# A hybrid RWKV-7 / mixture-of-experts trunk: gate/up weight pieces by rows in place of by columns

## The reference, cut to what matters

```
gate, up = jnp.split(xb @ w_e_in[e], 2, axis=-1)     # xb: 128 x 1024, w_e_in[e]: 1024 x 1024
return (jax.nn.silu(gate) * up) @ w_e_out[e]         # w_e_out[e]: 512 x 1024
```

## Time and profile before

| | us |
|---|---|
| median of 3 runs | 4692.15 (4687.72 to 4694.24) |
| the profiled execution: its time | 4703.23 |
| the profiled execution: its span | 4701.5 |
| expert stage in it: first weight piece issued | 3439.5 |
| expert stage in it: first gate/up matmul | 3478.96 |
| expert stage in it: last down product begins | 4596.52 |

### The profile page before, as it was taken

One profiled execution on the slowest core, in us unless ns is written; L12 is line 12 of the kernel. 1 busy time (PEld: TensorE's weight loads), 2 busy tenths in 40 slices (PEclk: granted clock), 3 DMA queues, 4 the chain that ended last, 5 costly groups with the idle time before them and its releaser, 6 DMA issues.

```text
span 4701.5 us, 91708 instructions
## 1 busy us (share of the span) xinstructions
PE 4270.4 (91%) x36691; PEld 2267.5 (48%) x36691; DVE 1599.4 (34%) x3167; ACT 1308.9 (28%) x2960; POOL 322.2 (7%) x422
## 2 busy tenths in 40 slices
PE   6999999999999999999999999989859999999991
PEld 4455555555555555555555555555434444444440
DVE  3333443343344344433434433332341111111115
ACT  4123333333333333333333333333301111011115
POOL 0000100010000001000000100000000000000004
PEclk8999999999999999999999999999869999999995
DMA  9101000100100100100100100033269999999998
GB/s 309 52 8 35 23 11 24 34 9 16 40 13 9 47 8 13 48 8 13 46 11 8 50 11 8 8 127 125 89 236 398 398 397 398 398 397 398 398 397 327
DMA packets 316735, 628.36 MB, mean 134 GB/s; under 512 B 11602, under 2 KB 96820, under 8 KB 316340
## 3 DMA queue, kind: packets, MB, share of 16 engines
q1 hardware_dynamic: 297908, 555.52, 32.6%
q0 software_dynamic: 11520, 41.95, 2.3%
q10 hardware_dynamic: 6912, 25.17, 1.3%
HBM read 561.75 MB, written 60.84 MB: 132 GB/s over the span
## 4 chain that ended last, share of the span: by engine, by line
PE 85%; issue 6%; DVE 4%; DMA 2%; ACT 2%; SPq 1%; POOL 1%; DVEq 0%; POOLq 0%; ACTq 0%
PE bank L962 38%; PE bank L1296 9%; PE bank L1300 5%; PE bank L1176 5%; PE bank L1326 5%; PE duo L1087 4%; PE bank L1330 2%; PE duo L1076 2%; PE duo L1074 1%; PE duo L1280 1%; ACT xs L1362 1%; PE bank L1019 1%; PE duo L899 1%; DMA yb<-y_s,dix 1%; PE bank L1003 1%
## 5 line engine op out<-in xcount | busy, mean ns | idle before, releaser
L962 PE MATMUL bank<-hT,w 128*128 (+1 forms) x4096 | 1792.6, 594 | 0.0
L962 PEld LDWEIGHTS bank<-hT,w 128*128 128x128 f32 x4096 | 778.1, 191 | 996.5 <-issue 996.5
L1296 PE MATMUL bank<-W,xT 128*128 128x512 f32 x1024 | 447.1, 595 | 2.2 <-DVE xT L2201 1.5
L1362 ACT ACT_TABLE_LOAD x268 | 343.8, 1283 | 21.0 <-DVE ub L1920 14.3
L1296 PEld LDWEIGHTS bank<-W,xT 128*128 128x128 f32 x1024 | 192.8, 191 | 233.7 <-issue 233.7
L1300 PE MATMUL bank<-W,xT 128*64 128x512 f32 x1024 | 241.3, 627 | 40.1 <-issue 40.1
L2207 DVE TENSOR_TENSOR gsig<-bank,gsig 128x512 f32<-128x512 f32 x48 | 33.2, 691 | 709.7 <-ACT gsig L1362 709.7
L727 POOL TENSOR_TENSOR Tm<-Tm,idents 128x512 f32<-128x512 f32 x32 | 40.5, 1267 | 2837.0 <-DVE Tm L1953 2837.0
L1176 PE MATMUL bank<-wo,mT 128*128 128x512 f32 x512 | 233.6, 602 | 0.0
L1326 PE MATMUL bank<-W,aT 128*128 128x512 f32 x512 | 225.1, 592 | 0.0
L1362 ACT ACTIVATE gsig<-bank 128x512 f32<-128x512 f32 x48 | 28.7, 597 | 694.7 <-PE bank L1296 423.9
(11 more groups left out here) (366 smaller groups left out, 5533.9 us busy)
## 6 DMA issues: line engine op xcount, KB each, us to landing
W<-in_w_expert_in_dram SPq DMA_DIRECT2D x128, 2048.0 KB, 21.5
W<-in_w_expert_out_dram SPq DMA_DIRECT2D x64, 2048.0 KB, 21.1
w<-in_w_in_dram SPq DMA_DIRECT2D x64, 512.0 KB, 3.9
adaw<-in_w_ada_dram SPq DMA_DIRECT2D x12, 2048.0 KB, 12.9
y_s<-ysb ACTq DMA_DIRECT2D x48, 512.0 KB, 6.7
xt<-in_x_dram SPq DMA_DIRECT2D x16, 512.0 KB, 8.7
WAc<-rank_s SPq DMA_DIRECT2D x32, 256.0 KB, 3.3
GDc<-rank_s SPq DMA_DIRECT2D x32, 256.0 KB, 3.2
```

The costliest lines, as they stand in the source:

```text
L962: ins = mm(PJ[j % 2][:, :], w[:, j, k, :], hT[:, k, ds(group(i) * G, G)], start=k == 0, stop=k == KT - 1)
L1296: ins = mm(GU[half][:, :], xT[:, slot, k, :], ring_in(parts[0])[:, k, :], start=k == 0, stop=k == KT - 1)
L1362: return nc.scalar.activation(o, i, f, **kw)
```

## The change

Each gate/up piece now holds half of the rows in full width: the first piece rows 0 to 511, the second rows 512 to 1023, 4 KB each. The number of pieces, their size, the order of issue, the ring and its slots stay. PE's order inside `gate_up` follows: with the first piece it runs k tiles 0 to 3 of the gate and then k tiles 0 to 3 of up, with the second piece k tiles 4 to 7 of both. The semaphore of the first piece gets another name.

```diff
-        def ring_in(r):
-            return ring(r).rearrange("p (k n) -> p k n", n=DE)
-        def ring_out(r):
+        def ring_rows(r):
             return ring(r).rearrange("p (k n) -> p k n", n=D)
...
-            def in_half(half):
-                return lambda r, e: (ring_in(r), e_in[0, ds(e, 1), :, half * DE:half * DE + DE]
-                                     .rearrange("e (k p) n -> p (e k) n", p=P))
+            def rows_in(part):
+                rows = slice(part * (D // 2), part * (D // 2) + D // 2)
+                return lambda r, e: (ring_rows(r), e_in[0, ds(e, 1), rows, :].rearrange("e (k p) n -> p (e k) n", p=P))
...
-                for half in range(2):
-                    parts = gate_part(s, half)
+                for part in range(2):
+                    parts = in_part(s, part)
                     for r in parts:
                         pe.wait_ge(ring_sem[r % RING], ring_full(h, r))
                     pe.sem_inc(S["pair_go"])
-                    for k in range(KT):
-                        if len(parts) == 1:
-                            ins = mm(GU[half][:, :], xT[:, slot, k, :], ring_in(parts[0])[:, k, :],
-                                     start=k == 0, stop=k == KT - 1)
...
-                    ins.then_inc(S["gu_done"] if half else S["gate_done"], 1)
+                    for half in range(2):
+                        cols = slice(half * DE, half * DE + DE)
+                        for k in range(KT // 2):
+                            kk_ = part * (KT // 2) + k
+                            if len(parts) == 1:
+                                ins = mm(GU[half][:, :], xT[:, slot, kk_, :], ring_rows(parts[0])[:, k, cols],
+                                         start=kk_ == 0, stop=kk_ == KT - 1)
+                            else:
+                                for lane, r in zip(LANE, parts):
+                                    ins = mm(GU[half][lane, :], xT[:, slot, kk_, lane], ring_rows(r)[:, k, cols],
+                                             start=kk_ == 0, stop=kk_ == KT - 1)
+                    ins.then_inc(S["gu_done"] if part else S["first_rows_done"], 1)
```

More of the change, by code:

```diff
@@ L99, in build @@
         shifted operands gates branch km_step rn_step P_step hats rs_step yc_step post_step conv_step sumsq
-        ln_done rstd tr_done T_act T_dve index_col chain patterns ada_trip pair_go gate_done""".split()
+        ln_done rstd tr_done T_act T_dve index_col chain patterns ada_trip pair_go first_rows_done""".split()
         S = {n: ctx.enter_context(nc.semaphore(n)) for n in names}
@@ L362, in ring_full, with in_part @@
             return 16 * (h * 3 + r // RING + (0 if r % RING in (2, 3) else 1)) + RING_BASE
-        def gate_part(s, half):
+        def in_part(s, part):
             base, j = 12 * (s // 3), s % 3
-            return [base + 4 * j + half] if j < 2 else [base + 7 + 2 * half, base + 8 + 2 * half]
+            return [base + 4 * j + part] if j < 2 else [base + 7 + 2 * part, base + 8 + 2 * part]
         def down_part(s):
@@ L617, in _ @@
             for s in range(6):
-                for half, signal in ((0, "gate_done"), (1, "gu_done")):
-                    for r in gate_part(s, half):
+                for part, signal in ((0, "first_rows_done"), (1, "gu_done")):
+                    for r in in_part(s, part):
                         OWNER[r] = (signal, s)
@@ L639, in fill @@
                 sp.dma_start(*source(r, e)).then_inc(ring_sem[r % RING], 16)
-            def in_half(half):
-                return lambda r, e: (ring_in(r), e_in[0, ds(e, 1), :, half * DE:half * DE + DE]
-                                     .rearrange("e (k p) n -> p (e k) n", p=P))
+            def rows_in(part):
+                rows = slice(part * (D // 2), part * (D // 2) + D // 2)
+                return lambda r, e: (ring_rows(r), e_in[0, ds(e, 1), rows, :].rearrange("e (k p) n -> p (e k) n", p=P))
             def rows_out(r, e):
-                return (ring_out(r), e_out[0, ds(e, 1), :, :].rearrange("e (k p) n -> p (e k) n", p=P))
+                return (ring_rows(r), e_out[0, ds(e, 1), :, :].rearrange("e (k p) n -> p (e k) n", p=P))
             def load_block(h, s, down=True):
-                for half in range(2):
-                    for r, column in zip(gate_part(s, half), experts_of(h, s)):
-                        fill(h, r, column, in_half(half))
+                for part in range(2):
+                    for r, column in zip(in_part(s, part), experts_of(h, s)):
+                        fill(h, r, column, rows_in(part))
                 if down:
@@ L1325, in down @@
                         if len(parts) == 1:
-                            ins = mm(Y2[j][:, :], aT[:, slot, k * P:k * P + P], ring_out(parts[0])[:, k, cols],
+                            ins = mm(Y2[j][:, :], aT[:, slot, k * P:k * P + P], ring_rows(parts[0])[:, k, cols],
                                      start=k == 0, stop=k == DE // P - 1)
@@ L1329, in down @@
                             for lane, r in zip(LANE, parts):
-                                ins = mm(Y2[j][lane, :], aT[:, slot, k * P:k * P + P][:, lane], ring_out(r)[:, k, cols],
+                                ins = mm(Y2[j][lane, :], aT[:, slot, k * P:k * P + P][:, lane], ring_rows(r)[:, k, cols],
                                          start=k == 0, stop=k == DE // P - 1)
```

## The result

The changed kernel takes 4650.73 us (median of 4 runs, 4647.93 to 4656.95) against 4693.19 us before (4 runs): ratio 0.9912, 95% interval 0.9899 to 0.9925. In two later comparisons the ratio was 0.9933 (0.9918 to 0.9948) and 0.9932 (0.9917 to 0.9948). The three differences of medians are 42.5, 32.8 and 33.1 us, 36 on average. The profiled execution has a span of 4649.9 us.

A forecast was written before the change was run, and what follows sets the result against it. The prediction took the DMA engines to bound the expert stage; 121 gate/up pieces at 0.304 us less give 36.8 us, all other terms 0, so 4692.15 - 37 = 4655 us. Its own range was 4649 to 4660, the wider one 4642 to 4678.

The forecast's parts named there:

- The DMA engines set the pace of the stage: Expert stage: three blocks move 28.3 MB, 71.1 us at 398 GB/s, the measured period, with PE 7% behind.
- A piece is 0.304 us cheaper, and 121 pieces count: 36.8 us: Gate/up pieces: 4 KB rows at 410 GB/s for 2 KB at 387; 121 of 128 pieces count, 36.8 us saved.
- Rival 1: Gate/up transfers: only part of the rate difference belongs to row size; smaller gain of 15 us, 4677 us, chance 0.14.
- Three blocks in 68.8 us: Late in the expert stage, the period of three blocks falls from 71.2 to 68.8 us, still above PE's 66.34.
- the forecast's 408 to 412: Expert stage: sign that the DMA rate rises to 408 to 412 GB/s in place of 398.
- The first wait near 3925 us: Pair blocks: first wait near 3925 us, not 3727, and later waits of 1.5 to 3 us.
- The last gate/up half near 4544 us: End of the expert stage: the last gate/up half starts near 4544 us in place of 4580.78.
- PE's order costs 0: Gate/up matmuls: changing bank after 4 k tiles in place of 8 and reading 512 of 1024 columns costs 0.
- ScalarE's and VectorE's steps: After gate/up: the sigmoid already waits for both products, so nothing moves: 0.
- SyncE: Issue of the pieces: half the descriptors per piece can only let it issue earlier; 0.
- Rival 3: Gathers land late against 4 KB packets, deciding only beyond 19.9 us; at 21 us the kernel takes 4708; chance 0.03.
- Rival 4: Expert stage: 4 KB rows run at 414 everywhere and slow matmuls behind waits go; 4637 to 4645 us, chance 0.08.

The follow-up runs named there:

- e5: Changed kernel with half of each gate/up piece left out and the loaded half used twice: 4632.11 us, ratio to before 0.9861.
- e6: Kernel before with half of each gate/up piece left out and the loaded half used twice: 4638.13 us, ratio to before 0.9867.
- e1: The changed kernel unedited, timed in more rounds against the kernel before: 4660.45 us, ratio 0.9933.
- e10: The changed kernel unedited, timed once more against the kernel before: 4661.76 us, ratio 0.9932.
- e3: Changed kernel, two transfers per piece, those of gate/up splitting the columns so runs are 2 KB again: 4693.80 us, ratio to before 1.0008.
- e4: Kernel before with two transfers per piece, each gate/up transfer a quarter of the columns, runs of 1 KB: 4766.02 us, ratio to before 1.0167.
- e2: Changed kernel with every 2 MB piece, down too, moved by two 1 MB transfers, rows still 4 KB: 4657.68 us, ratio to before 0.9931.
- e9: Changed kernel with gate/up runs of 16 KB and the tokens' columns in matching order, products right: 4635.00 us, ratio to before 0.9876.
- e7: Changed kernel with gate/up runs of 16 KB, tokens' columns not reordered, so products wrong: 4643.06 us, ratio to before 0.9879.

## Why the prediction was right

The forecast was 4655 us with a gain of 37; measured were 4650.73 with the first gain of 42.5, and 36 over three comparisons. The two later gains, 32.8 and 33.1, lie at the low edge of the forecast's own 33 to 43. That the first one lies 5.5 above the forecast and the mean within 1 is in part luck; the stage, which repeats better, is the firmer test. Step by step:

- *The DMA engines set the pace of the stage.* Shown by e5 and e6: take their bytes away and the pair blocks stop waiting. One reading on the way was off: the rate of 398 fills slices 31 to 39 of the earlier trace rows, not 27 to 39, whose first four have 89 to 236. Nothing in the sum rests on it.
- *A piece is 0.304 us cheaper, and 121 pieces count: 36.8 us.* The stage is 36.8 us shorter in the first profile, 36.1 in those of e1 and e10; that the first agrees to the last digit is chance. e3 takes the gain back with nothing but the run length, and e4 carries it on to 1 KB. Rival 1, a part of the rate's difference that isn't the row size, is out. The Trainium skill's 3 cycles a packet (DMA: Bandwidth & Descriptors, section Bandwidth) are too few for this cost, by e4's 73 us against an estimate of 31. The same section names 32 bytes of descriptor metadata per transfer as a second part of the penalty, which the prediction left out; as an estimate, one more cycle a packet would make e4 some 40 us slower, still not 73. By e2 and e3 it is neither the region nor the number of transfers.
- *Three blocks in 68.8 us.* 68.9. The rate is 411 GB/s, inside the forecast's 408 to 412.
- *The first wait near 3925 us.* It came at 3910.73 in an execution whose stage began 14.5 us earlier, so at 3925 with the start of before. Of the nine later waits seven are 2.3 to 2.5 us, as forecast; two are 0.50 and 0.16. Only the one at 4187.11 is followed by slower matmuls (8.78 us for 7.09).
- *The last gate/up half near 4544 us.* 4529.45, or 4544 with that start.
- *PE's order costs 0.* Shown by e5 against e6. ScalarE's and VectorE's steps did not move.
- *SyncE.* The prediction had only "can issue earlier", and its consequence was left out: SyncE now runs into the ring. Its waits for slots between 3500 and 4500 went from 12, together 41.5 us, to the 33 below, 150.9 us, and a piece takes 25.5 us from issue to landing where it took 21.4. That more bytes stand in the queue would explain both; it was not tested. It cost nothing, as the DMA share is 1.03 in all three stretches shown above. What SyncE's issues waited for in the changed kernel, to be read against the earlier trace rows:

```profile
SPq L635 <- PE bank L1295: 50.6, 13, 6.0
SPq L635 <- PE bank L1299: 42.2, 9, 6.4
SPq L635 <- PE bank L1325: 36.2, 7, 6.6
SPq L635 <- PE bank L1329: 21.9, 4, 6.8
```

- *Rival 3, late gathers.* Their landing is unchanged, 5.9/7.5/9.6 us against 5.9/7.6/9.1, in the changed kernel's view of tile xg:

```profile
DMA to landing us min/median/max: 5.9/7.5/9.6
```

- *Rival 4, a larger gain.* The slow matmuls behind the waits did shrink (the line's busy time fell from 241.3 to 227.2 us, its idle time from 40.1 to 18.0, 36 us together), but 4 KB rows run at 411 and not at 414, and while the DMA is the bound a faster PE only waits longer. The larger gain needs longer runs, as e9 shows.

The first comparison's 42.5 us are more than the stage gave. The stage's start varies by some 20 us from execution to execution, in code that is the same in all eleven, and medians of a few runs can carry part of that.

## What to carry to other kernels

When a stream of weights keeps all DMA engines busy, look for windows of a few us in which only one kind of transfer is in flight, and compare their rates: they price a new layout before it is built. Then find how far the next bound is. Here PE's floor was 58 us away, row halves took 37 of it and runs of 16 KB the rest, and past that a faster transfer is worth nothing in this stage.

## What the runs showed of the hardware

- A packet costs about 9.7 ns and 37.5 ns per KB on one of the 16 DMA engines: 348, 387, 410 and 429 GB/s for runs of 1, 2, 4 and 16 KB, each in windows with that kind alone (e4, before, the changed kernel, e7 and e9). In e9, 4 KB packets went at 415 to 424, which this line does not cover.
- A run of 16 KB that is contiguous on both sides travels as one packet; the count of packets fell by exactly three quarters of those of the gate/up pieces.
- Splitting each 2 MB transfer into two of 1 MB cost about 1 us over 192 more transfers (stage 1088.7 us against 1087.2 to 1087.9), with the rate at 411 GB/s as before.
- VectorE's tensor_scalar over 1024 columns took 1.28 us with its output in steps of 512 bytes (e9), and 0.75 us without (the changed kernel).
